# A float32 decoder trunk: high and low activation halves in one 512-column matmul, output groups in two parts

## The reference

```python
h = h + hgrn2_mixer(rms_norm(h, w0), ...)       # layer 0: proj = xn @ w_in (2048 x 8192), gated recurrence, @ w_out (2048 x 2048)
h = h + conv_glu_ffn(rms_norm(h, w1), ...)      # u = causal_dwconv(xn @ w_up (2048 x 11264)); (silu(gate) * val) @ w_down (5632 x 2048)
h = h + short_conv_mixer(rms_norm(h, w2), ...)  # layer 1: proj = xn @ w_in (2048 x 6144); gb * conv(gc * h) @ w_out
h = h + conv_glu_ffn(rms_norm(h, w3), ...)
return rms_norm(h, final_norm)
```

## Time and profile before

| | us |
|---|---|
| median of 3 runs | 2440.34 (2439.85 to 2440.71) |
| profiled execution, span from first to last instruction | 2437.6 |
| PE busy | 2417.2 (99%) |
| DVE busy | 1607.2 (66%) |
| ACT busy | 964.0 (40%) |
| weights and x loaded by SP's queue | 432.62 MB, 59.3% of 16 DMA engines |

### The profile page before, as it was taken

The page is one execution under the profiler, slowest core; times in us unless marked ns, Lnnn a source line. Parts: engine busy times, 40 slices in busy tenths (PEclk is TensorE's granted clock), DMA queues, the critical chain, the costliest instruction groups (busy, mean ns, idle before and its releaser), DMA issues.

```text
span 2437.6 us, 47938 instructions
## 1 busy us (share of the span) xinstructions
PE 2417.2 (99%) x18883; PEld 2357.5 (97%) x18883; DVE 1607.2 (66%) x1937; ACT 964.0 (40%) x975; POOL 5.4 (0%) x10
## 2 busy tenths in 40 slices
PE   8999999999999999999999999999999999999998
PEld 8999999999999999999999999999999999998886
DVE  6767777767767777764445666566777777776443
ACT  6342333444343333334444333344433333443443
POOL 0000000000000000000000000000000000000000
PEclk9999999999999999999999999999999999999999
DMA  7565655465666665655565565556656656665664
GB/s 222 150 168 143 167 140 162 137 199 174 189 181 178 186 183 176 189 182 183 183 185 180 184 185 174 190 181 183 182 180 186 181 182 183 181 198 182 192 196 147
DMA packets 225485, 435.36 MB, mean 179 GB/s; under 512 B 13344, under 2 KB 14176, under 8 KB 225248
## 3 DMA queue, kind: packets, MB, share of 16 engines
q1 hardware_dynamic: 224896, 432.62, 59.3%
q10 hardware_dynamic: 480, 1.18, 0.1%
HBM read 431.65 MB, written 2.10 MB: 178 GB/s over the span
## 4 chain that ended last, share of the span: by engine, by line
PE 99%; DMA 0%; ACT 0%; ACTq 0%; DVE 0%; issue 0%; SPq 0%
PE acc L985 27%; PE acc L987 27%; PE acc L988 27%; PE acc L978 4%; PE acc L980 4%; PE acc L979 4%; PE side L1054 2%; PE side L1024 0%; PE side L941 0%; PE side L1048 0%; DMA x_tok<-in_x 0%; PE side L952 0%; PE side L1060 0%; DMA rows<-in_hgrn_out_norm 0%; ACT h L441 0%; ACT ta L429 0%
## 5 line engine op out<-in xcount | busy, mean ns | idle before, releaser
L487 DVE TENSOR_TENSOR w_lo<-raw,w_hi 128x1024 fp32r<-128x1024 f32 x816 | 995.4, 1224 | 757.2 <-ACT w_hi L307 747.6
L307 ACT ACTIVATE w_hi<-raw 128x1024 fp32r<-128x1024 f32 x816 | 862.4, 1059 | 1363.9 <-PE acc L988 1138.3
L985 PE MATMUL acc<-xn,w_hi 128*128 128x256 f32 x4352 | 1234.9, 284 | 0.0
L988 PE MATMUL acc<-xn,w_lo 128*128 128x256 f32 x4352 | 1231.9, 283 | 0.0
L987 PE MATMUL acc<-xn,w_hi 128*128 128x256 f32 x4352 | 1231.9, 283 | 0.0
L985 PEld LDWEIGHTS acc<-xn,w_hi 128*128 128x128 f32 x4352 | 835.7, 192 | 0.6
L987 PEld LDWEIGHTS acc<-xn,w_hi 128*128 128x128 f32 x4352 | 835.8, 192 | 0.2
L988 PEld LDWEIGHTS acc<-xn,w_lo 128*128 128x128 f32 x4352 | 835.6, 192 | 0.0
L985 PE MATMUL acc<-act,w_hi 128*128 128x256 f32 x1216 | 344.5, 283 | 0.0
L988 PE MATMUL acc<-act,w_lo 128*128 128x256 f32 x1216 | 344.1, 283 | 0.0
L987 PE MATMUL acc<-act,w_hi 128*128 128x256 f32 x1216 | 344.1, 283 | 0.0
(11 more groups left out here) (128 smaller groups left out, 1015.4 us busy)
## 6 DMA issues: line engine op xcount, KB each, us to landing
raw<-in_ffn_w_up SPq DMA_DIRECT2D x352, 512.0 KB, 4.3
raw<-in_ffn_w_down SPq DMA_DIRECT2D x176, 512.0 KB, 4.3
raw<-in_hgrn_w_in SPq DMA_DIRECT2D x128, 512.0 KB, 3.8
raw<-in_sc_w_in SPq DMA_DIRECT2D x96, 512.0 KB, 3.9
raw<-in_hgrn_w_out SPq DMA_DIRECT2D x32, 512.0 KB, 3.7
raw<-in_sc_w_out SPq DMA_DIRECT2D x32, 512.0 KB, 4.0
x_tok<-in_x SPq DMA_DIRECT2D x4, 512.0 KB, 7.2
out<-h SPq DMA_DIRECT2D x4, 512.0 KB, 4.1
```

The source lines that it names most:

```text
L307: nc.scalar.activation(w_hi[:, c % RING], raw[:, c % RING], ACT.Copy).then_inc(hi_ready, 1)
L487: v.tensor_tensor(w_lo[:, c % RING], raw[:, c % RING], w_hi[:, c % RING].bitcast(F32), ALU.subtract).then_inc(lo_ready, 1)
L985: mm(to[:, j, :], hi, src[:, t, 0, :], start=begin and j % 2 == 0, stop=False, skip_group_check=True)
L988: o = mm(to[:, j, :], lo, src[:, t, 0, :], start=False, stop=end, skip_group_check=True)
```

## The change

The high halves of a weight tile now meet both activation halves in one matmul: `features` streams the 512 columns [high | low] of a tile of `xn` or `act` against the high weights, and then the 256 high columns against the low weights. An output tile therefore has a whole PSUM bank: columns 0 to 255 hold high x high, and columns 256 to 511 hold the sum of the two small products. A set of `acc` is now two such banks, so a group is worked as two parts of 256 output features (GW), each over all input features, in chunks of KW = 4 input tiles by 256 features: again 512 KB, now from rows of 1 KB. At a part's end ACT copies the small sums out of PSUM (`correction`, to `corr`), DVE adds them to the large ones (`corrected`, to ta, tb or pad in SBUF) and frees the set; at a group's end `scaled` multiplies in SBUF. Where no norm is pending (DOWN0, SC_OUT) DVE adds both halves to h in two instructions. The residual work is done by parts, high parts before squares. The V group does the same with tokens on the partitions (`tokens`; its weights lie as [high | low] in `w_parts`). DOWN1 keeps its three 512-column matmuls and its chunks (`parts=1`, `wide_tokens`). In the first group of a phase with 8 chunks a group, the two parts are interleaved by the order in `steps`; SP now writes out the first iteration of every phase. The squares, the residuals and `ready` are counted by parts.

The diff, cut to its core:

```diff
+KW = 4
+TW = 2
+GW = TW * P
...
+    def __init__(self, before, n, groups, k_tiles, scales=0, corrects=True, parts=2):
+        self.n, self.groups, self.cpg, self.parts = n, groups, k_tiles // KC, parts
+        self.cpi, self.api = groups * self.cpg, groups * parts
+        self.scales, self.corrections = scales, self.api if corrects else 0
         self.c0 = before.c0 + before.n * before.cpi if before else 0
-        self.g0 = before.g0 + before.n * before.groups if before else 0
-        assert self.cpi % RING == 0 and self.c0 % RING == 0 and groups % SETS == 0
-HGRN_IN = Phase(None, 4, 4, DT)
+        self.a0 = before.a0 + before.n * before.api if before else 0
+        self.scaled0 = before.scaled0 + before.n * before.scales if before else 0
+        self.corr0 = before.corr0 + before.n * before.corrections if before else 0
+        assert self.cpi % RING == 0 and self.c0 % RING == 0 and self.api % SETS == 0
...
+    def steps(self, first, g):
+        if self.parts == 1:
+            order = [(0, k) for k in range(self.cpg)]
+        elif first and g == 0 and self.cpg == 8:
+            order = [(0, 0), (0, 1), (1, 0), (0, 2), (1, 1), (0, 3), (1, 2), (1, 3)]
+        else:
+            order = [(part, k) for part in range(2) for k in range(self.cpg // 2)]
+        last = self.cpg // self.parts - 1
+        return [(part, k, k == 0, k == last) for part, k in order]
...
+HGRN_IN = Phase(None, 4, 4, DT, scales=3)
 HGRN_OUT = Phase(HGRN_IN, 2, 2, DT)
-UP0 = Phase(HGRN_OUT, 11, 2, DT)
-DOWN0 = Phase(UP0, 2, 2, FT)
-SC_IN = Phase(DOWN0, 2, 6, DT)
-SC_OUT = Phase(SC_IN, 2, 2, DT)
-UP1 = Phase(SC_OUT, 11, 2, DT)
-DOWN1 = Phase(UP1, 2, 2, FT)
+UP0 = Phase(HGRN_OUT, 11, 2, DT, scales=2)
+DOWN0 = Phase(UP0, 2, 2, FT, corrects=False)
+SC_IN = Phase(DOWN0, 2, 6, DT, scales=6)
+SC_OUT = Phase(SC_IN, 2, 2, DT, corrects=False)
+UP1 = Phase(SC_OUT, 11, 2, DT, scales=2)
+DOWN1 = Phase(UP1, 2, 2, FT, corrects=False, parts=1)
...
-        raw = sb("raw", [P, RING, KC, GC])
-        w_hi = sb("w_hi", [P, RING, KC, GC], F32R)
-        w_lo = sb("w_lo", [P, RING, KC, GC], F32R)
+        raw = sb("raw", [P, RING, KW, GW])
+        w_parts = sb("w_parts", [P, RING, KW, 2, GW], F32R)
+        corr = sb("corr", [P, TW, T])
...
-        acc = ctx.enter_context(nc.psum_tensor("acc", [P, SETS, TG, T], F32))
+        acc = ctx.enter_context(nc.psum_tensor("acc", [P, SETS, TW, 2 * T], F32))
...
-        def rows_of(w, kk, col):
-            return w[kk * KC * P:(kk + 1) * KC * P, bass.ds(col, GC)].rearrange("(k p) n -> p k n", p=P)
+        def rows_of(phase, w, k, part, col):
+            if phase.parts == 1:
+                return w[k * KC * P:(k + 1) * KC * P, bass.ds(col, GC)].rearrange("(k p) n -> p k n", p=P)
+            return w[k * KW * P:(k + 1) * KW * P, bass.ds(col + part * GW, GW)].rearrange("(k p) n -> p k n", p=P)
+        def raw_slot(phase, c):
+            if phase.parts == 1:
+                return raw[:, c % RING].rearrange("p a n -> p (a n)").rearrange("p (k n) -> p k n", k=KC)
+            return raw[:, c % RING]
...
-                        for kk in range(phase.cpg):
+                        for kk, (part, k, _, _) in enumerate(phase.steps(first, g)):
...
-                            sp.dma_start(raw[:, c % RING], rows_of(w, kk, column(i, g))) \
+                            sp.dma_start(raw_slot(phase, c), rows_of(phase, w, k, part, column(i, g))) \
                                 .then_inc(w_loaded[c % RING], 16)
-                if phase is HGRN_IN:
-                    loop(sp, phase, body)
-                else:
-                    with sp.Fori(0, phase.n) as i:
-                        body(i, False)
+                loop(sp, phase, body)
...
-                nc.scalar.activation(w_hi[:, c % RING], raw[:, c % RING], ACT.Copy).then_inc(hi_ready, 1)
+                nc.scalar.activation(w_parts[:, c % RING, :, 0, :], raw[:, c % RING], ACT.Copy).then_inc(hi_ready, 1)
+            def correction(i, phase, g, part, c):
+                act_e.wait_ge(chunk_used, at(i, phase.cpi, c + 1 + RING))
+                a = g * phase.parts + part
+                act_e.wait_ge(acc_free, at(i, phase.api, phase.a0 + a + SETS))
+                if phase is HGRN_IN and g == V_GROUP:
+                    for b in range(T // P):
+                        o = nc.scalar.activation(corr[:, b, :], acc[:, a % SETS, b, T:], ACT.Copy,
+                                                 scale=rs[:, T + b:T + b + 1])
+                else:
+                    o = nc.scalar.activation(corr[:], acc[:, a % SETS, :, T:], ACT.Copy)
+                o.then_inc(corr_ready, 1)
...
+                            if ends and phase.corrections:
+                                correction(i, phase, g, part, c)
...
+            def residual(i, r, part, tile, weight):
+                act_e.wait_ge(h_ready, at(i, 4, r + part + 1))
+                high_parts(tile + part * TW, weight, TW)
+                nc.scalar.activation(ta[:, part * TW:(part + 1) * TW, :], h[:, bass.ds(tile + part * TW, TW), :],
+                                     ACT.Square).then_inc(sq_ready, 1)
...
-            def scaled(i, phase, g, dst):
-                dve.wait_ge(chunk_used, at(i, phase.cpi, phase.c0 + (g + 1) * phase.cpg + RING))
-                v.tensor_tensor(dst, acc[:, g % SETS], rs[:, None, 0:T].to_broadcast([P, TG, T]), ALU.mult) \
-                    .then_inc(acc_free, 1)
-            def await_scaled(i, phase, g):
-                dve.wait_ge(acc_free, at(i, phase.groups, phase.g0 + g + 1 + SETS))
+            def corrected(i, phase, g, part, dst):
+                a = g * phase.parts + part
+                dve.wait_ge(corr_ready, at(i, phase.corrections, phase.corr0 + a + 1))
+                if phase is HGRN_IN and g == V_GROUP:
+                    for b in range(T // P):
+                        o = v.scalar_tensor_tensor(
+                            out=vt[:, part * TW:(part + 1) * TW, b, :],
+                            in0=acc[:, a % SETS, b, 0:T].rearrange("p (c d) -> p c d", d=P), scalar=rs[:, T + b:T + b + 1],
+                            in1=corr[:, b, :].rearrange("p (c d) -> p c d", d=P), op0=ALU.mult, op1=ALU.add)
+                else:
+                    o = v.tensor_tensor(dst[:, part * TW:(part + 1) * TW, :], acc[:, a % SETS, :, 0:T],
+                                        corr[:], ALU.add)
+                o.then_inc(acc_free, 1)
+            def await_corrected(i, phase, g):
+                dve.wait_ge(acc_free, at(i, phase.api, phase.a0 + (g + 1) * phase.parts + SETS))
+            def scaled(i, phase, g, n, dst):
+                await_corrected(i, phase, g)
+                v.tensor_tensor(dst, dst, rs[:, None, 0:T].to_broadcast([P, TG, T]), ALU.mult) \
+                    .then_inc(scaled_ready, 1)
+            def await_scaled(i, phase, n):
+                dve.wait_ge(scaled_ready, at(i, phase.scales, phase.scaled0 + n + 1))
...
+            def normed(i, phase, r, sq, part, tile, weight):
+                low_parts(i, 4, r + part, tile + part * TW, weight, TW)
+                add_squares(i, 4, sq + part, sq + part, ta[:, part * TW:(part + 1) * TW, :])
...
+                    r, sq = (n0 + g * phase.parts for n0 in (r0, sq0))
+                    if rs_n is not None and kk == phase.cpg - 1:
+                        await_corrected(i, phase, g)
+                        link(v.tensor_tensor(tb[:], tb[:], rs[:, None, 0:T].to_broadcast([P, TG, T]), ALU.mult), i)
+                        for part in range(phase.parts):
+                            dst = h[:, bass.ds(tile + part * TW, TW), :]
+                            v.tensor_tensor(dst, dst, tb[:, part * TW:(part + 1) * TW, :], ALU.add).then_inc(h_ready, 1)
+                        for part in range(phase.parts):
+                            dve.wait_ge(h_ready, at(i, 4, r + part + 1))
+                            normed(i, phase, r, sq, part, tile, weight)
+                    elif rs_n is None and ends:
+                        a = g * phase.parts + part
+                        c = phase.c0 + g * phase.cpg + kk
+                        dst = h[:, bass.ds(tile + part * TW, TW), :]
+                        dve.wait_ge(chunk_used, at(i, phase.cpi, c + 1 + RING))
+                        link(v.tensor_tensor(dst, dst, acc[:, a % SETS, :, 0:T], ALU.add), i)
+                        v.tensor_tensor(dst, dst, acc[:, a % SETS, :, T:], ALU.add).then_inc(h_ready, 1)
+                        dve.wait_ge(h_ready, at(i, 4, r + part + 1))
                         v.sem_inc(acc_free, 1)
-                    add_squares(i, 2, sq0 + g, ta)
-                    low_parts(i, 2, r0 + g, tile, weight)
-                phase_of(phase, pieces)
+                        normed(i, phase, r, sq, part, tile, weight)
+                phase_of(phase, pieces, into=lambda g: tb)
...
+            def features(to, c, src, k, begin, end):
+                w = w_parts[:, c % RING]
+                for q in range(KW):
```

(58 more changed lines are left out.)

131 lines of the change are left out of this document (63 added, 68 removed).

## The result

The changed kernel took 2408.27 us (median of four runs, 2407.47 to 2410.01), the kernel before 2440.53 us beside it: a ratio of 0.9869, 95% interval 0.9855 to 0.9883. The change makes it faster, by 32 us and not by the 66 forecast, and 2408 lies outside the range of 2366 to 2398. The profiled execution took 2408.16 us with a span of 2406.3 us.

The account below looks back on a forecast made before the run. PE was taken to bound the kernel, by the number of matmuls times their spacing. From 2437.6 us, -74.2 + 1.7 + 3.5 + 2.2 + 0.5 gave a 2371.3 us span, or 2374.0 us measured; range 2366 to 2398.

Parts of the forecast that it names:

- feature tiles: In the feature groups, one 512-column matmul replaces two of 256: 13.3 ns less for each of 5568 tiles, -74.2 us.
- V group: In the first phase's V group, two halves of 512 + 256 columns replace three 512-column matmuls: +1.7 us.
- waits at the start: In the first phase's first group, PE waits 1.2 and 2.3 us for x groups needed earlier: +3.5 us.
- wait on act in HGRN_OUT: At the sixth chunk of HGRN_OUT, PE waits for the last group of act: +2.2 us, 1 to 4.
- ends of groups: At the group ends of HGRN_OUT, weight splits come late behind the residual work: +0.5 us, 0 to 3.
- Rival A: At part ends PE waits for the new evictions: 2599 us, 3%; a smaller form, 2398 to 2435 us, 6%.
- Rival B: Weight loads in 1 KB pieces make DMA the bound, each costing 110 ns like a 2 KB one: 2790 us, 2%.
- 60 to 70%: Sign of a right forecast: DMA share of 60 to 70%, with the landing under 6 us.
- Rival C: In the feature groups the dropped matmul is worth little: 2448 us, or about 2434 by the skill's page; 3%.
- 16 matmuls of a chunk in 2.77 us: Sign of a right forecast: PE starts the 16 matmuls of a chunk in 2.77 us.
- 2.88: Sign of a wrong forecast: a chunk takes 2.88 us, so the dropped matmul is worth only a little.

Follow-up runs that it names:

- E6: One 64-column float32 dummy matmul added to the changed kernel at the end of each of the five sum-of-squares stages: 2377.29 us, ratio 0.9742.
- E7: The changed kernel with ACT's copy of the small products made twice at every part's end but the V group's: 2407.53 us, ratio 0.9866.
- E5: The changed kernel with another order in a phase's first group, both parts using each quarter of the inputs in turn: 2413.47 us, ratio 0.9888.

## Why the prediction was wrong, by its steps

**The step that failed** is the first term: "A feature tile costs 3 x 120.0 = 360.0 ns now and 226.7 + 120.0 = 346.7 ns after". The mechanism is right, an overhead of 13.3 ns goes with a matmul, and 346.7 is what a pair takes in the fast rhythm; but 4920 of the 5568 tiles ran in the slow one, at 353.3. That is 4920 x 6.7 ns = 33 us of the 74 given back, and E6 got 31 of them back by one small matmul in each of five stages. The prediction had said that a mixed stream is not in the trace, and then took the price from two pure streams, as if a price could have only one value; its range reached to a third of the term lost, and 44% was.

All the terms, in us of span, beside what the traces show:

```
term                     forecast   measured
feature tiles              -74.2      -41.4   (-74.2 + 32.8)
V group                     +1.7       +2.0   (48 of its 256 pairs slow)
waits at the start          +3.5       +6.5   (below)
wait on act in HGRN_OUT     +2.2       +1.6
ends of groups              +0.5        0
sum                        -66.3      -31.3   (span 2437.6 to 2406.3: -31.3)
```

The measured tile and V terms are counts of tiles by their spacing, the others are read from the timeline; that the sum meets the span to 0.1 us is in part luck, for by single phases it is off by up to 0.3.

**The start** cost more. Its rows in the timeline of PE, with the wait in HGRN_OUT as the last:

```profile
19.52 0.50 PE L1035 MATMUL acc<-xn,w_parts 128*128 128x512 f32 x1 [0.76 <-DVE xn L597]
...
29.16 0.80 PE L1035 MATMUL acc<-xn,w_parts 128*128 128x512 f32 x1 [2.85 <-DVE xn L597]
29.76 0.41 PE L1037 MATMUL acc<-xn,w_parts 128*128 128x256 f32 x1
29.97 0.63 PE L1035 MATMUL acc<-xn,w_parts 128*128 128x512 f32 x1
...
466.88 0.50 PE L1035 MATMUL acc<-act,w_parts 128*128 128x512 f32 x1 [1.63 <-DVE act L845]
```

The waits themselves are near the forecast's 1.2 and 2.3 us. What it left out is that PE came back from the second at half its clock: from 29.20 to 31.00 the window's granted clock is 0.50.

```profile
29.20:31.00 1.80, 1.80 (x5) 1.55 (x6) 1.77 (x3) 1.80 (x3) 0.00 (x0) 0.50 0.06 11
```

The first eight chunks took 32.1 us and 26.6 before, 26.2 if each is 0.05 shorter: 5.9 us, and the first matmul stands at 13.82, 0.6 us later than before (13.4 to 13.9 in the other kernels); 6.5 in all. Of the 5.9, 3.6 are waits and 1.5 the lower clock (the five pairs behind the second wait took 3.3 us in place of 1.8); the rest is not told apart.

**Rival A** (evictions exposed), 9% in both forms: wrong. No wait at a part's end; DVE is 80% busy in UP0, as forecast (82%), ACT 1041 us over the run (1070 forecast; the copy takes 0.58 us and not 0.65, and the 16 part ends of DOWN0 and SC_OUT have none). E7 doubled the copy for nothing. The window of the earlier trace rows in the changed kernel:

```profile
565.00:800.00 235.00, 235.00 (x1332) 203.69 (x1331) 187.88 (x256) 104.22 (x112) 0.00 (x0) 1.00 0.61 185
```

It did show up where the order makes two parts end together behind other work (E5), a case that the prediction had not looked at.

**Rival B** (1 KB pieces): wrong. 411264 packets keep 16 engines busy 58.3% of 2406.3 us, 55 ns each, the lower of the two estimates (55 and 60); landing is 3.9 us after issue (4.3 before). It was said that 60 to 70% would show, a little too much.

**Rival C** (the dropped matmul is worth little) was given 3% and by itself is wrong too, but it held the half that came true: in the slow rhythm exactly half of the 13.3 ns stays with the tile (353.3 = 346.7 + 6.7). By the Trainium skill (TensorE: Matmul & The Clock Gate, "Wait — 56ns, not 53.3ns?") matmuls follow each other after N / 2.4 GHz and some 2.5 ns; by that a pair would take 325 ns, an estimate from the page. The trace does not agree in either rhythm, with 346.7 and 353.3, and E6 shows that leaving out one matmul of three saves 13.3 ns in the fast rhythm.

What would show it right was named as "16 matmuls of a chunk in 2.77 us", and wrong as 2.88. The chunk of 2.83 us lies between, and that one number points at the failed term.

## What to carry to other kernels

A price read from a uniform stream is a forecast for a mixed one, not its cost: where a change mixes shapes on the engine that bounds the kernel, give that term a range of its own, and read the spacing over a whole cycle at several places of the trace afterwards. If the same instructions run at two spacings in two places, try a small foreign instruction, or a grouped order, before more work is cut; here the one gave 31 us and the other 23. Which foreign instruction helps must be tried: 64 columns against a full weight tile did here, and against half a tile did not. When an order is changed to avoid a wait on inputs, check also where the outputs then end: two accumulators that end together need their evictions at once.
